# One 4 MB load instead of two 2 MB loads for each expert's second weight, with the first weight's columns read in strided groups

## What is computed

```
combine = sum(one_hot(top_idx, 32) * gates, axis=-2)        # 4 of 32 experts per token
for e in range(32):
    z = h @ w1[e] + b1[e]                                   # 1024 -> 2048
    glu = minimum(z[..., 0::2], 7)
    lin = clip(z[..., 1::2], -7, 7)
    act = glu * sigmoid(1.702 * glu) * (lin + 1)            # 1024 values
    out += combine[..., e] * (act @ w2[e] + b2[e])          # 1024 -> 1024
```

## Time and profile before

| | |
|---|---|
| median of three executions | 1101.18 us (1098.81 to 1102.26) |
| the profiled execution | 1099.66 us, of which the recorded span is 1097.9 us |
| TensorE matmuls busy | 1047.8 us, 95% of the span |
| VectorE, ScalarE busy | 290.1 us (26%), 175.2 us (16%) |
| moved by DMA | 430.14 MB, mean 392 GB/s |
| mean granted TensorE clock | 0.976 of full speed |

### The profile page before, as it was taken

One profiled execution on the slowest core, in us unless ns is written; L12 is line 12 of the kernel. 1 busy time (PEld: TensorE's weight loads), 2 busy tenths in 40 slices (PEclk: granted clock), 3 DMA queues, 4 the chain that ended last, 5 costly groups with the idle time before them and its releaser, 6 DMA issues.

```text
span 1097.9 us, 11722 instructions
## 1 busy us (share of the span) xinstructions
PE 1047.8 (95%) x4652; PEld 402.2 (37%) x4652; DVE 290.1 (26%) x710; ACT 175.2 (16%) x310; POOL 21.0 (2%) x27
## 2 busy tenths in 40 slices
PE   8999899999999999899998989998999898999995
PEld 7458354333333333233332323332333333333331
DVE  2565634222121212121211212121313122211222
ACT  1231322111111111111111111111111111011112
POOL 1202000000000000000000000000000000000000
PEclk9999998999999999999999989998999999999998
DMA  9787816999999999999999999999999999999993
GB/s 331 189 301 285 364 39 267 398 435 426 432 427 435 430 431 431 429 433 426 433 429 432 429 435 425 430 430 432 430 432 436 427 432 429 435 427 433 423 427 157
DMA packets 34135, 430.14 MB, mean 392 GB/s; under 512 B 5068, under 2 KB 6496, under 8 KB 16032
## 3 DMA queue, kind: packets, MB, share of 16 engines
q1 hardware_dynamic: 32256, 426.44, 92.2%
q10 hardware_dynamic: 1216, 1.70, 1.1%
q0 software_dynamic: 640, 1.69, 0.5%
HBM read 427.19 MB, written 2.62 MB: 391 GB/s over the span
## 4 chain that ended last, share of the span: by engine, by line
PE 72%; DMA 25%; DVE 1%; ACT 1%; SPq 1%; issue 0%; DVEq 0%; ACTq 0%
PE ps L1226 30%; DMA w1r<-w_mlp 22%; PE ps L1257 14%; PE ps L1273 6%; PE ps L991 4%; PE ps L1196 3%; PE ps L979 3%; DMA w2r<-w_mlp 2%; PE ps L1113 1%; PE ps L1038 1%; PE ps L1144 1%; PE ps L1204 1%; PE ps L1234 1%; PE ps L1103 1%; DMA w1r<-w_in 1%; PE ps L1281 1%
## 5 line engine op out<-in xcount | busy, mean ns | idle before, releaser
L1226 PE MATMUL ps<-w1r,arena 128*64 128x512 f32 x2048 | 489.9, 614 | 24.3 <-DMA w1r<-w_mlp 24.3
L1226 PEld LDWEIGHTS ps<-w1r,arena 128*64 128x64 f32 x2048 | 140.1, 140 | 292.9 <-issue 259.7
L1257 PE MATMUL ps<-w2r,arena 128*64 128x512 f32 x992 | 218.6, 592 | 3.9 <-DMA w2r<-w_mlp 3.9
L1257 PEld LDWEIGHTS ps<-w2r,arena 128*64 128x64 f32 x992 | 71.1, 137 | 140.0 <-issue 130.6
L901 DVE TENSOR_TENSOR acc<-ps,acc 128x512 f32<-128x512 f32 x64 | 41.2, 686 | 230.4 <-PE ps L1273 230.4
L893 DVE TENSOR_TENSOR arena<-arena 128x512 f32<-128x512 f32 x32 | 22.1, 692 | 172.8 <-ACT arena L548 172.8
L557 ACT ACTIVATE arena<-ps 64x512 f32<-64x512 f32 x32 | 18.9, 592 | 296.4 <-PE ps L1257 296.4
L857 DVE TENSOR_SCALAR sel_z<-small 96x64 bf16 (+1 forms) x32 | 6.1, 191 | 225.6 <-PE ps L1226 225.6
L1273 PE MATMUL ps<-arena 128*128 128x512 f32 x128 | 63.2, 617 | 1.3 <-ACT arena L559 1.3
L1196 PE MATMUL ps<-h,arena 128*64 128x512 f32 x248 | 58.5, 592 | 0.0
L871 DVE TENSOR_SCALAR arena<-small,rank,gate 128x64 f32<-128x64 f32 x128 | 31.3, 307 | 62.9 <-PE ps L1281 62.9
(11 more groups left out here) (230 smaller groups left out, 574.6 us busy)
## 6 DMA issues: line engine op xcount, KB each, us to landing
w1r<-w_mlp SPq DMA_DIRECT2D x54, 4096.0 KB, 31.6
w2r<-w_mlp SPq DMA_DIRECT2D x62, 2048.0 KB, 19.6
w1r<-w_mlp SPq DMA_DIRECT2D x19, 2048.0 KB, 11.7
w1r<-w_in SPq DMA_DIRECT2D x7, 2048.0 KB, 18.5
w1r<-w_mlp SPq DMA_DIRECT2D x6, 1024.0 KB, 6.8
w1r<-w_out SPq DMA_DIRECT2D x2, 2048.0 KB, 13.7
rel_table<-arena ACTq DMA_DIRECT2D x1, 1536.0 KB
acc<-x SPq DMA_DIRECT2D x2, 512.0 KB, 4.4
```

Of the source, the lines that this page charges most:

```text
L1226: ins = mm(ps[64 * c:64 * c + 64, 2 * par + n, :], hgT[:, par, k % 4, 64 * (k // 4):64 * (k // 4) + 64], w1r[:, 8 * par + k, at:at + 512], ...
L1257: ins = mm(ps[at:at + 64, 4 + c, :], actT[:, k % 4, 64 * (k // 4):64 * (k // 4) + 64], (w1r if last else w2r)[:, k // 2, col:col + 512], s ...
```

## The change

w2 is laid out as `e (p j) d` with eight rows per partition: partition p holds rows 8p to 8p + 7, one run of 32 KB. For experts 1 to 30 it is loaded by a single 4 MB transfer that is issued when `down(e-1)` has finished all eight blocks, and `down(e)` waits for all of it ahead of k = 0. w2(0) and w2(31) keep their pieces, with other source addresses. To match, hidden unit 8q + 4c + j goes to half c, so both bias and w1 are read as 64 groups of eight neighbouring columns, sixteen columns apart. Sizes and number of products stay.

```diff
-        w2_v = w_mlp2[0].rearrange("e (c p j) d -> e c p (j d)", c=2, p=P)
+        w2_v = w_mlp2[0].rearrange("e (p j) d -> e p (j d)", p=P)
...
-            def load_w2(e, c):
-                sp.dma_start(w2r[:, 2 * c:2 * c + 2, :].rearrange("p a f -> p (a f)"), w2_v[e, c]).then_inc(w2_in[c], 16)
+            def load_w2_half(c):
+                sp.dma_start(w2r[:, 2 * c:2 * c + 2, :].rearrange("p a f -> p (a f)"), w2_v[0, :, 4096 * c:4096 * c + 4096]).then_inc(w2_in[c], 16)
...
             def next_w2(base, e):
-                for c in range(2):
-                    sp.wait_ge(w2_used, 4 * base + (4 * (e - 1) + 2 * c + 2))
-                    load_w2(e, c)
+                sp.wait_ge(w2_used, 4 * base + (4 * (e - 1) + 4))
+                sp.dma_start(w2r[:, :, :].rearrange("p a f -> p (a f)"), w2_v[e]).then_inc(w2_in[0], 16)
...
-                sp.dma_start(w1r[:, 0:2, :].rearrange("p a f -> p (a f)"), w2_v[NE - 1, 0]).then_inc(w2_last[0], 16)
+                sp.dma_start(w1r[:, 0:2, :].rearrange("p a f -> p (a f)"), w2_v[NE - 1, :, 0:4096]).then_inc(w2_last[0], 16)
...
-                        at = 1024 * c + 512 * n
-                        mm(ps[64 * c:64 * c + 64, 2 * par + n, :], sel_z[:, par, :], bias3[:, at:at + 512], start=True, stop=False)
+                        cols_z = bias3[:, 1024 * n:1024 * n + 1024].rearrange("p (q s) -> p q s", s=16)[:, :, 8 * c:8 * c + 8]
+                        mm(ps[64 * c:64 * c + 64, 2 * par + n, :], sel_z[:, par, :], cols_z, start=True, stop=False)
...
-                        at = 1024 * c + 512 * n
+                        cols_z = w1r[:, 8 * par + k, 1024 * n:1024 * n + 1024].rearrange("p (q s) -> p q s", s=16)[:, :, 8 * c:8 * c + 8]
                         ins = mm(ps[64 * c:64 * c + 64, 2 * par + n, :], hgT[:, par, k % 4, 64 * (k // 4):64 * (k // 4) + 64],
-                                 w1r[:, 8 * par + k, at:at + 512], start=False, stop=(k == 7))
+                                 cols_z, start=False, stop=(k == 7))
...
-                    if not last and k % 4 == 0:
-                        pe.wait_ge(w2_in[k // 4], 16 * wb + 16 * (e + 1))
+                    if not last and k == 0:
+                        pe.wait_ge(w2_in[0], 16 * wb + 16 * (e + 1))
+                    if k == 4 and isinstance(e, int) and e == 0:
+                        pe.wait_ge(w2_in[1], 16)
```

More of the change, by code:

```diff
@@ L276, in _ @@
             for c in range(2):
-                load_w2(0, c)
+                load_w2_half(c)
             sp.wait_ge(proj_done, 7)
@@ L306, in next_w2 @@
             def next_w2(base, e):
-                for c in range(2):
-                    sp.wait_ge(w2_used, 4 * base + (4 * (e - 1) + 2 * c + 2))
-                    load_w2(e, c)
+                sp.wait_ge(w2_used, 4 * base + (4 * (e - 1) + 4))
+                sp.dma_start(w2r[:, :, :].rearrange("p a f -> p (a f)"), w2_v[e]).then_inc(w2_in[0], 16)
             def last_w2(base):
                 sp.wait_ge(w1_used, 8 * base + 8 * (NE - 2) + 2)
-                sp.dma_start(w1r[:, 0:2, :].rearrange("p a f -> p (a f)"), w2_v[NE - 1, 0]).then_inc(w2_last[0], 16)
+                sp.dma_start(w1r[:, 0:2, :].rearrange("p a f -> p (a f)"), w2_v[NE - 1, :, 0:4096]).then_inc(w2_last[0], 16)
                 sp.wait_ge(w1_used, 8 * base + 8 * (NE - 2) + 4)
                 for i in range(2):
-                    sp.dma_start(w1r[:, 2 + i, :], w2_v[NE - 1, 1, :, 2048 * i:2048 * i + 2048]).then_inc(w2_last[1 + i], 16)
+                    sp.dma_start(w1r[:, 2 + i, :], w2_v[NE - 1, :, 4096 + 2048 * i:6144 + 2048 * i]).then_inc(w2_last[1 + i], 16)
             def rest_of_sweep(base):
```

## The result

The changed kernel took 1103.82 us (median of 20 executions, 1101.23 to 1108.89) against 1101.31 us (20 executions): ratio 1.0027, 95% interval 1.0018 to 1.0037. The forecast was 1105.6 us, 0.40% slower, with a range of 1100.8 to 1111.0. The profiled execution after has a span of 1100.7 us against 1097.9.

A forecast was written before the change was run, and what follows sets the result against it. The DMA queue paces the kernel to about 990 us, then TensorE alone. Terms: -1.8 (transfers) + 1.9 (empty queue) + 3.0 (whole w2(30)) + 1.3 (clock) = +4.4 us, giving 1105.6 us; range 1100.8 to 1111 us.

The forecast's parts named there:

- The saving of a merged load: w2 transfers in the queue: longer runs save 0.06 us each, 1.8 us over 30 experts, bounds -0.9 and 2.7.
- The issue of w2(5): Queue at w2(5): issued at 335.3 us against a limit of about 335.5 us, so it just holds.
- The empty queue at w2(11): Queue before w2(11): late issue leaves 0.2 us empty, plus 1.7 us for the clock, 1.9 us in all.
- The end: down(30) needs all of w2(30): starts at 1068.9 us, 3.1 us later than before; 3.0 us in the sum.
- The clock at the end: Behind TensorE's 2.8 us wait at down(30): lower clock costs 1.3 us, bounds 0 and 1.7.
- nothing behind down(30) gives time back: Last experts: down(31) needs its data only at 1075.75 us and later, so no delay is recovered.
- The strided read: z and bias products reading groups of eight columns: taken as costing nothing; as a rival, chance 0.10.
- Rival A: Whole kernel stays within 3.3 us: no clock loss at down(9) or down(30), +1.4 us, 1102.6 us; chance 0.36.
- My forecast's case: Whole kernel slower by +3.3 to +9 us, 1104.5 to 1110 us; chance 0.50.
- the four waits named as signs: TensorE's timeline: down(3), down(4), down(9) and down(10) would show waits at k = 0.

The follow-up runs named there:

- e3: Kernel before, old layout, both w2 pieces issued where they were but both awaited ahead of block 0 of down(e): ratio 1.0021, 1103.72 us.
- e5: Changed kernel with w2(1) to w2(10) in two pieces, issued and awaited as before the change, later loads merged: ratio 1.0017, 1103.57 us.
- e1: Changed kernel with w2 again in two 2 MB pieces, issued and awaited as before the change, new layout kept: ratio 0.9995, 1101.51 us.
- the two repetitions: The changed kernel itself, unaltered, measured twice more beside other runs: ratio 1.0055, 1105.93 us, and ratio 1.0055, 1105.23 us.
- e11: The changed kernel itself, unaltered, measured again beside the version with pieces at both ends: ratio 1.0055, 1105.23 us.
- e4: Changed kernel with only w2(29) and w2(30) in two pieces, issued and awaited as before the change: ratio 0.9986, 1099.19 us.
- e9: Changed kernel with z products reading every second column of w1, output not the layer's: ratio 1.0053, 1105.61 us.
- e8: Changed kernel with z products reading every fourth column of w1, output not the layer's: ratio 1.3939, 1534.8 us.

## Why the prediction was right, step by step

- **The saving of a merged load**, taken as 0.06 us with bounds -0.03 and 0.09, was 0.08 us by the landings after, 2.4 us for 30 loads instead of 1.8.
- **The issue of w2(5)** was put at 335.3 us and came at 335.3; down(4) was put at about 328.1 and came at 328.04 us. As computed, the limit just held, or nearly: 0.2 us of queue were empty. The times are right, but the step behind them is not: down(4) did not wait for w2(4), which had landed at 305.8 + 22.0 = 327.8 us. It was late because down(3) had waited 2.48 us for w2(3) and began at 298.68 instead of 295.86 us. Both delays are close to 2.9 us, which was luck.
- **The empty queue at w2(11)**: the issue was put at 500.9 us plus 1.7 us for the clock behind down(9)'s wait, and came at 502.8. down(9) waited 4.30 us and took 8.78. The empty time, put at 1.9 us, was 1.86. e3 keeps the wait and the clock but not the late issue, and e5 keeps the merge but not the late start of down(9); in both the queue does not run dry. The cause is therefore the pair of both, as argued.
- **The end** was too low: down(30) was put at 1068.9 us and came at 1070.34. The missing 1.4 us are at w2(29). It was issued at 1021.7 with work still queued, but landed at 1040.9 us, 11.3 us behind the second half of w1(30) (issued at 989.6, 40.1 us to landing, 1029.7) instead of 9.7. The prediction had no such term. The 0.6 us more of savings and some smaller delays in the row of landings nearly cancel.
- **The clock at the end** was too high: 1.3 us were added for down(30), whose wait of 2.28 us cost 0.05. In addition down(31) ran 1.7 us faster than in the profile before, where the prediction had said that nothing behind down(30) gives time back. It is not shown to be luck of one execution: down(31) took 8.73 us in e1 too, which loads and waits as the kernel before, and 7.03 or 7.04 us in the other nine traces of versions that compute the layer. Over all executions the mean clock was 0.971 to 0.979 for the kernel before and 0.976 to 0.985 for the changed one. Why it falls at down(31) in the first and not in the second is open. The two errors of the end, +1.4 and -1.3, cancel by luck, and the third stands: 4.4 + 1.4 - 1.3 - 1.7 = 2.8 us, the difference of the spans.
- **The strided read** was taken as free, and is: e1.
- **Rival A** (within 3.3 us) holds the result's median, 2.5 us up, though not by A's conditions: the clock was lost at down(9) and held at down(30). My forecast's case, +3.3 us and more, holds the two repetitions, whose medians are 4.7 and 5.7 us up. The mechanism is the same in both. Why the medians of whole sets differ by 2 to 3 us is open: the spans of the three traces are within 2 us, e11 has its 1.9 us more for the most part from ahead of the landing of w2(1) (at 241.6 us instead of 239.9), and the clock behind the waits differs from one execution to the next.
- Of the four waits named as signs, those of down(3) and down(9) came. down(4) and down(10) had none: the delay of the `down` before them brought TensorE there after its data, at 495.57 us in the case of down(10).

## What to carry to other kernels

When two resources are both nearly full, ask of a later or coarser load two things: how much is queued ahead of it when it is issued (here 12.1 us from issue to landing for 4 MB was the limit), and whether it stands behind the last wait that the other resource has. At the first place lateness costs nothing up to the limit and is paid beyond it, at the second it is paid in full. A merged transfer of the same bytes saved 0.08 us; the half that it no longer delivered early cost 3 us once. Split the loads where lateness counts; to merge the others gained at most 0.17% here, and one of its two sets is not clear of nothing.

## What was not expected of the hardware

- One transfer of w2 in the last experts landed 1.35 to 1.55 us behind its place in the row of landings, in the changed kernel's three traces (w2(29)), although the queue was full. The part of the transfer that finished last was late, the first was not: of the 16 signals of its landing the first came 9.7 us behind that of the load ahead, the last 11.3. It is no matter of the merge: in e4, where w2(29) comes in pieces, the first of them is 1.5 us late as well. In the profile before nothing of the kind stands there, but its first and last signals are 2.6 us apart already, against 0.55 in the profile after just ahead of w2(29). The cause is not settled; nothing was tried for it.
- The clock behind a short wait is not set by its length. Behind the 2.19 us wait at 990.86 us sixteen products took 5.35 us, behind the 2.28 us wait at 1070.34 us they took 3.65, in the same execution. Of its waits of 2.19 us, the one that ended at 641.20 us was followed by sixteen products in 3.65 us. Such a term can be given as a chance only.
- Two reads out of 16 bytes cost a float32 product of 512 columns 3%, and one read 82% (e9, e8).
